# Ten instead of six of a layer's 24 gate tiles beside the attention's heads

## The reference

```
h = rmsnorm(x, norm1_g)
P = h @ w_in                                   # 1024 -> RWKV | attention | retention | gate columns
P_rw, P_sa, P_ret, P_gate = split_cols(P, ...)
y_rw  = rwkv_mixer(P_rw, ...)                  # time mixing: a recurrence over the tokens, 8 heads of 64
y_sa  = dsa_mixer(P_sa, ...)                   # attention: 8 heads over at most 256 (144) chosen keys
y_ret = retention_mixer(P_ret, ...)
gates = sigmoid(P_gate).reshape(B, L, 3, 1024) # 3072 gate columns: 24 tiles of 128
merged = (gates[:, :, 0] * (y_rw @ w_br_rwkv) + gates[:, :, 1] * (y_sa @ w_br_dsa)
          + gates[:, :, 2] * (y_ret @ w_br_ret))
x = x + merged @ w_o
x = x + square(relu(rmsnorm(x, norm2_g) @ w_up)) @ w_down
```

## Time and profile before

| what | value |
|---|---|
| runs (median, range) | 2645.03 us (2640.41 to 2651.56) |
| the profiled execution | 2640.55 us |
| its span | 2638.4 us |
| PE busy | 2540.2 us, 96% |
| DVE, ACT, POOL busy | 1224.3, 579.8, 1347.1 us |
| granted TensorE clock, mean | 0.985 |
| heads of blocks 0 to 3, layer 0 | about 252 to 440 us |
| block 4 and preparation, layer 0 | about 440 to 527 us |
| the six bodies, layer 0 | about 527 to 753 us |

### The profile page before, as it was taken

One profiled execution on the slowest core, in us unless ns is written; L12 is line 12 of the kernel. 1 busy time (PEld: TensorE's weight loads), 2 busy tenths in 40 slices (PEclk: granted clock), 3 DMA queues, 4 the chain that ended last, 5 costly groups with the idle time before them and its releaser, 6 DMA issues.

```text
span 2638.4 us, 62410 instructions
## 1 busy us (share of the span) xinstructions
PE 2540.2 (96%) x24614; PEld 2372.9 (90%) x24614; DVE 1224.3 (46%) x2244; ACT 579.8 (22%) x1147; POOL 1347.1 (51%) x1780
## 2 busy tenths in 40 slices
PE   7998999899989999999999989998999899999998
PEld 7997888789969999999999878887999699999998
DVE  5357885545455422121443578755454553221224
ACT  3122222312132211011220222223112332110112
POOL 6634443412227766666775444433221377666665
PEclk9999999999999999999999989999999999999999
DMA  5212112211135222222242211122111442222221
GB/s 194 97 49 76 62 51 88 106 40 40 40 136 175 81 82 87 80 87 79 82 148 67 72 59 65 58 86 91 44 46 43 154 159 81 82 88 80 87 79 68
DMA packets 67689, 223.76 MB, mean 85 GB/s; under 512 B 8736, under 2 KB 9632, under 8 KB 66432
## 3 DMA queue, kind: packets, MB, share of 16 engines
q1 hardware_dynamic: 45360, 160.46, 18.2%
q10 hardware_dynamic: 22096, 59.95, 6.7%
HBM read 190.25 MB, written 29.03 MB: 83 GB/s over the span
## 4 chain that ended last, share of the span: by engine, by line
PE 89%; DVE 4%; DVEq 2%; issue 1%; ACT 1%; DMA 1%; ACTq 1%; POOL 0%; POOLq 0%
PE dense L539 72%; PE mix L539 15%; DVEq L1569 2%; PE mix L958 1%; ACT in_hi L1077 0%; DMA region_b<-region_b 0%; DVE region_b L2018 0%; POOL w_lo L526 0%; DVE x L1855 0%; ACT region_b L1077 0%; PE dense L958 0%; DVE act_lo L1587 0%; DVE region_b L2022 0%; ACTq L1150 0%; ACT y_mix L1077 0%
## 5 line engine op out<-in xcount | busy, mean ns | idle before, releaser
L522 POOL TENSOR_SCALAR w_hi<-w_raw 128x512 fp32r<-128x512 f32 x592 | 374.5, 651 | 1245.8 <-PE dense L539 966.0
L526 POOL TENSOR_TENSOR w_lo<-w_raw,w_hi 128x256 fp32r<-128x256 f32 x1184 | 972.6, 851 | 24.7
L539 PE MATMUL dense<-act_hi,w_hi 128*128 128x288 f32 x2272 | 688.1, 314 | 26.1 <-POOL w_lo L526 12.9
L539 PE MATMUL dense<-in_hi,w_hi 128*128 128x288 f32 x2432 | 678.6, 294 | 9.5 <-DVE in_lo L2079 8.7
L539 PE MATMUL dense<-in_lo,w_hi 128*128 128x288 f32 x2432 | 678.3, 295 | 0.0
L539 PE MATMUL dense<-act_lo,w_hi 128*128 128x288 f32 x2272 | 651.6, 298 | 0.0
L539 PE MATMUL dense<-act_hi,w_lo 128*128 128x288 f32 x2272 | 537.8, 298 | 0.0
L539 PE MATMUL dense<-in_hi,w_lo 128*128 128x288 f32 x2432 | 522.2, 296 | 0.0
L539 PEld LDWEIGHTS dense<-act_hi,w_hi 128*128 128x128 f32 x2272 | 433.6, 191 | 83.6 <-issue 56.6
L539 PEld LDWEIGHTS dense<-in_hi,w_hi 128*128 128x128 f32 x2432 | 458.7, 189 | 10.9 <-DVE in_lo L2079 8.9
L539 PEld LDWEIGHTS dense<-in_lo,w_hi 128*128 128x128 f32 x2432 | 458.9, 189 | 0.0
(11 more groups left out here) (200 smaller groups left out, 2523.0 us busy)
## 6 DMA issues: line engine op xcount, KB each, us to landing
w_raw<-in_stream SPq DMA_DIRECT2D x296, 512.0 KB, 3.2
y_mix<-gate_scratch ACTq DMA_DIRECT2D x48, 288.0 KB, 3.0
gate_scratch<-region_b ACTq DMA_DIRECT2D x36, 288.0 KB, 2.2
x_scratch<-x ACTq DMA_DIRECT2D x2, 2304.0 KB, 12.5
y_scratch<-y_mix ACTq DMA_DIRECT2D x2, 2304.0 KB, 10.0
x<-x_scratch ACTq DMA_DIRECT2D x2, 2304.0 KB, 10.1
y_mix<-y_scratch ACTq DMA_DIRECT2D x2, 2304.0 KB, 9.1
gate_scratch<-region_a ACTq DMA_DIRECT2D x12, 288.0 KB, 2.1
```

Source lines behind the costliest of these rows:

```text
L522: hi = nc.gpsimd.tensor_scalar(w_hi[:, v, c], w_raw[:, s, c], 1.0, 1.0, ALU.mult, ALU.mult)
L526: lo = nc.gpsimd.tensor_tensor(w_lo[:, v, c], w_raw[:, s, c], w_hi[:, v, c].bitcast(F32), ALU.subtract)
L539: return nc.tensor.matmul(out, lhsT, rhs, start=start, stop=stop, skip_group_check=True)
```

## The change

Four more gate tiles a layer are computed in the attention's runs: gate tiles 0 to 9 instead of 0 to 5. Blocks 0 to 2 have three slices behind the values instead of two, block 3 three ahead of them instead of two, so that each of the 32 runs has one slice more. The bodies have 60 slices instead of 92; `body_range` spreads them by the same shares. Nothing else differs.

```
-GATES_DSA = 6
+GATES_DSA = 10
 T_GATE_RW = T_GATE + GATES_DSA
-FILL_STEP = ((3, 2), (3, 2), (3, 2), (2, 2), (0, 0))
+FILL_STEP = ((3, 3), (3, 3), (3, 3), (3, 2), (0, 0))
```

## The result

The changed kernel took 2657.8 us (median of six runs, 2652.8 to 2660.7), the kernel before beside it 2647.7. The ratio is 1.0038 (95% interval 1.0020 to 1.0057): slower by 10 us, inside the range and inside the half per cent that the prediction counted as no change, but 2.3 times the 4.4 us of the sum. Run once more it was 1.0047 (1.0033 to 1.0062).

A forecast was written before the change was run, and what follows sets the result against it. PE was taken to bound heads and bodies. Heads +24.5, bodies -25.9, uncovered waits +3.6 gave +2.2 us a layer, +4.4 for both, on the 2645.03 us median: 2649 us; range 2638 to 2663.

The forecast's parts named there:

- rival 3: Bodies, level 4: ACT held by gate stores in every body, 6.7 us a layer more, 2662 us; chance 0.05.
- The heads: Attention runs: one slice more in each of 32 runs, 0.79 us each, adds 24.5 us a layer.
- The slice hidden in run 1: Heads, run 1: PE waits for DVE in any case, so the slice ahead costs nothing, 0.8 us off 25.3.
- rival 4: Heads: dense buffers come late and PE waits 1 us at half of 24 tiles, 2673 us; chance 0.05.
- the counted groups: Bodies: 29 groups go from two slices to one (22.9 us), three vanish (3.0 us); 25.9 us a layer removed.
- the uncovered waits: Bodies: waits that the missing slices no longer hide, 3.6 us a layer in all, bounds -2.2 to 10.3.
- Rivals 1 and 2: Bodies: 1, no wait appears, 2638 us, chance 0.14; 2, each slice also takes 0.2 us along, 2631 us, 0.04.
- The idle time ahead of body 0's turned products: Body 0: PE already waits 1.18 us for DVE, so the vanished group saves nothing; 1.0 us given back.
- the 0.79 less 0.26 of the sum: Turned products of bodies 1 and 2: a slice of 0.79 us goes, spare is 0.53, so 0.26 us each is uncovered.
- Removed here, added there: 0: Level 4: the 2.22 us wait for ACT's copy leaves body 0 and comes in body 1, net 0.
- Rival 5, the clock: Bodies: the clock falls at eight new waits a layer, 1.55 us each, 2674 us; chance 0.04.

The follow-up runs named there:

- both_hidden64: Changed kernel, one slice moved from body 2 to body 0's first stage, plus 64 semaphore increments spread over three PE waits: 2640.8 us, ratio 0.9986.
- early_tile: Changed kernel, one slice moved from body 2 to body 1, so gate tile 8 ends ahead of level 3's m1: 2648.0 us, ratio 1.0008.
- after_hidden64: Changed kernel plus 64 semaphore increments spread over three PE waits: 2657.5 us, ratio 1.0048; run again 2654.5 us, ratio 1.0045.
- cover: Changed kernel, one slice moved from body 1 to body 0, between the first and the turned products: 2652.1 us, ratio 1.0029.
- before_again: Kernel before, unaltered, a single execution for a second trace: 2640.0 us.

## Why the prediction was right, and where its sum was short

- **The time: inside the range, by the range's width.** The sum's 2649 us was 9 us short of 2657.8. The upper end of the range stood for rival 3, which did not happen; what did happen, a longer wait and late code, was in no bound.
- **The heads: right.** +25.2 us against +24.5. The slice hidden in run 1 was hidden: that wait shrank from 2.96 to 2.15. No wait on `dense_free` appeared; rival 4 is out.
- **The slices removed in the bodies: right.** With the level-4 wait gone and the gaps nearly so (both_hidden64) the bodies last 205.9 us, 26.0 less than before; the counted groups are 25.9, and the uncovered waits that stay would about make up for the level-4 wait of before. Rivals 1 and 2, bodies shorter by over 26 us, are out.
- **The idle time ahead of body 0's turned products: right.** 2.26 us, and the vanished group saved nothing. The turned products of body 1 came 0.53 us closer to the start of the body, the 0.79 less 0.26 of the sum.
- **The other uncovered waits: right.** By the lists above they grew by 3.2 us in layer 0, and by 3.0 to 3.2 in the two traces, against 3.6.
- **"Removed here, added there: 0": the step that failed.** It moved a wait of 2.22 us from one body to the other at its old length. A wait that DVE ends is as long as PE is early; one slice fewer stood ahead of it, DVE's own chain was half a us longer there (why was not tested), and it took 3.5 us. With the clock behind it (1.5 us in both layers) it cost 2.7 us a layer more than the sum has. The mechanism and the place were right (early_tile), the size was not.
- **No term for code.** Waits on "issue" rose from 0.5 to 3.1 us a layer on the mean of the traces. The kernel before shows one such gap of 0.7 us, on its list of waits, and I passed over it.
- **Rival 5, the clock: partly there,** at one place a layer for 1.5 us, not at eight for 1.55. Behind the level-4 wait of 3.5 us the small matmuls ran slowly in all ten layers that have it (two traces of the changed kernel, two of after_hidden64, one of cover; 0.57 and 0.50 in layer 0 of the first two). Behind waits of 2.1 to 2.3 us in body 0 they did so in three of sixteen, one of them in the kernel before (before_again, layer 1, 0.55), so the prediction's reading that such waits leave the clock alone holds for most executions and not for all. The Trainium skill (TensorE: Matmul & The Clock Gate, HAM oscillation) says that idle gaps bring the clock down to its lower level; body 1 agrees in both traces, body 0 in one of two.
- **Rival 3: out.** Level 4 waited in body 1 alone, by ACT's order, as forecast.

The two terms, 2.7 and 2.6 us, and what body 0 was short, where the clock comes and goes (0.6), are 5.9 of the 6.6 us. Since the other uncovered waits came out 0.5 us smaller than the sum has them, about 1 us is left that I can't place. Twice the net of the table, +8.8 us a layer, is 17.6 us; the runs say 10 to 12. Stretches that the change does not touch, from the first layer's group norm to the second's heads above all, last 802 to 812 us in the fourteen traces, so single traces can't settle that difference. For the same reason the 2.6 us a layer for code are a figure of the traces; that a placing of the code changes the median was not shown.

## What to carry to other kernels

A wait that a slow engine ends has a fixed end, not a fixed length: when work ahead of it is taken away, add that work to the wait, also where the wait only moves. When long and short instructions are mixed, the long ones can also buy time for loading the code of the short ones; look for waits on "issue" before thinning them out. And where a store is queued between an engine's urgent instructions, ask when its data is finished: here one slice moved, at no cost, was worth 6 to 8 us.

## What the runs showed of the hardware

PE's program came in blocks of 16 KB, one for some 246 matmuls and weight loads. PE stood still for 0.3 to 3.5 us where a block was late, and went on 1.23 to 1.52 us after it had landed, 50 times of 50. It stood most often in or just behind the rows of 64 by 64 matmuls with no wait between them. Shifting the program by 64 instructions without other work went with bodies 4 to 6 us a layer shorter in the traces of one kernel, and of another 4 to 6 us shorter in one layer and 2 to 4 us longer in the other. A semaphore increment on PE took 0.15 us.
